# Decoder step on one core: gathering only the selected rows of the paged cache, and ranking the blocks earlier

## The reference

```
o_cmp, p   = attend(q, compressed keys, compressed values)   # one key per block
imp        = sum of p over the 4 query heads of the kv head
score      = imp, with blocks 0, 31 and 32 forced to the top
idx        = top_k(score, 16)                                # 16 of 33 blocks
o_sel      = attend(q, sel_k of the blocks in idx, sel_v of the blocks in idx)
o_win      = attend(q, last 512 window keys, values)
o          = g0 * o_cmp + g1 * o_sel + g2 * o_win
```

## Time and profile before

| | |
|---|---|
| median of 3 runs | 1637.56 us (1637.17 to 1639.81) |
| the profiled execution | 1638.89 us |
| its span, first to last instruction | 1637.1 us |
| busy: TensorE / VectorE / ScalarE | 1351.6 / 592.1 / 281.6 us |
| moved by DMA | 591.24 MB, mean 361 GB/s |
| the samples' phase on TensorE (first key transpose to first `w_o` matmul) | 449.7 to 558.7 us |

### The profile page before, as it was taken

How to read it: one execution, slowest core, us unless ns; L and a number is a source line. 1 busy time by engine, 2 the same in 40 slices (tenths; PEclk the granted TensorE clock), 3 DMA queues, 4 the chain that set the end, 5 groups by cost and what they waited for, 6 DMA issues and landing times.

```text
span 1637.1 us, 24667 instructions
## 1 busy us (share of the span) xinstructions
PE 1351.6 (83%) x10647; PEld 844.7 (52%) x10647; DVE 592.1 (36%) x1289; ACT 281.6 (17%) x660; POOL 90.5 (6%) x112
## 2 busy tenths in 40 slices
PE   8999999999999899996866788667785676676675
PEld 6887888888866588643323243333332232232332
DVE  2845566686686221382401212012120120120125
ACT  0013301201265010211110111101111011011113
POOL 1220011011231000010000000000000000000000
PEclk9999999999999999997977988889898797897888
DMA  9975476887789999479999999999999999999996
GB/s 347 376 272 197 166 278 222 315 318 263 278 332 409 341 306 361 180 305 423 426 426 426 428 412 427 426 427 426 414 426 429 426 427 426 428 426 426 427 427 249
DMA packets 139874, 591.24 MB, mean 361 GB/s; under 512 B 9056, under 2 KB 98672, under 8 KB 106864
## 3 DMA queue, kind: packets, MB, share of 16 engines
q1 hardware_dynamic: 122624, 497.70, 76.5%
q0 software_dynamic: 10432, 75.82, 11.9%
q10 hardware_dynamic: 6704, 16.08, 2.6%
HBM read 580.54 MB, written 17.45 MB: 365 GB/s over the span
## 4 chain that ended last, share of the span: by engine, by line
PE 56%; DMA 41%; DVE 1%; ACT 1%; issue 1%; DVEq 0%; SPq 0%; ACTq 0%
DMA arena<-in_w_up 36%; PE ps L710 22%; PE ps L2251 9%; PE ps L1437 7%; PE ps L2269 3%; PE ps L2218 3%; DMA arena<-in_w_down 2%; PE ps L1280 2%; DMA arena<-in_win_v 2%; PE ps L860 1%; PE ps L2278 1%; PE ps L1289 1%; PE ps L2224 1%; ACT arena L1712 1%; PE ps L2148 0%
## 5 line engine op out<-in xcount | busy, mean ns | idle before, releaser
L2251 PE MATMUL ps<-arena 128*32 128x256 f32 x4352 | 338.9, 481 | 236.9 <-DMA arena<-in_w_up 236.7
L2251 PEld LDWEIGHTS ps<-arena 128*32 128x32 f32 x4352 | 183.4, 137 | 408.1 <-issue 362.2
L710 PE MATMUL ps<-arena 128*128 128x264 f32 x1600 | 365.4, 386 | 0.0
L710 PEld LDWEIGHTS ps<-arena 128*128 128x128 f32 x1600 | 299.9, 190 | 49.6 <-issue 0.9
L1969 DVE TENSOR_TENSOR arena<-arena,ps 64x256 f32<-64x256 f32 x34 | 14.4, 424 | 474.4 <-ACT arena L1716 474.4
L2269 PE MATMUL ps<-arena 128*32 128x512 f32 x1088 | 125.9, 602 | 1.6 <-DMA arena<-in_w_down 1.1
L1437 PE MATMUL ps<-arena 128*128 128x264 f32 x512 | 118.2, 388 | 1.3 <-DMA arena<-in_w_o 1.3
L1716 ACT ACTIVATE arena<-ps 64x256 f32<-64x256 f32 x34 | 12.8, 375 | 566.2 <-PE ps L2251 566.2
L1437 PEld LDWEIGHTS ps<-arena 128*128 128x128 f32 x512 | 95.8, 190 | 20.7 <-issue 3.4
L2218 PE MATMUL ps<-arena 128*32 128x512 f32 (+1 forms) x816 | 98.5, 595 | 0.1
L1729 ACT COPY arena<-ps 32x512 f32<-32x512 f32 x128 | 73.7, 576 | 134.6 <-PE ps L2269 122.2
(11 more groups left out here) (481 smaller groups left out, 1125.0 us busy)
## 6 DMA issues: line engine op xcount, KB each, us to landing
arena<-in_w_up SPq DMA_DIRECT2D x61, 2048.0 KB, 34.1
arena<-in_w_gate SPq DMA_DIRECT2D x59, 2048.0 KB, 31.1
arena<-in_w_down SPq DMA_DIRECT2D x59, 2048.0 KB, 31.2
arena<-in_w_in SPq DMA_DIRECT2D x50, 1024.0 KB, 10.3
arena<-in_w_o SPq DMA_DIRECT2D x16, 1024.0 KB, 11.0
arena<-in_w_gate SPq DMA_DIRECT2D x10, 1024.0 KB, 30.7
arena<-in_w_down SPq DMA_DIRECT2D x10, 1024.0 KB, 31.2
arena<-in_w_up SPq DMA_DIRECT2D x6, 1024.0 KB, 31.1
```

Of the source, the lines that this page charges most:

```text
L710: last = pe.matmul(ps[:, n % 2, 0:T], ring[:, slot, k, cols], x[:, k, :], start=(k == 0), stop=(k == KT - 1))
L2251: last = pe.matmul(ps[BS * q:BS * q + BS, 0, 0:CHUNK // 2], xs[:, kk * 4 + i, :], w[:, at:at + CHUNK // 2], start=(k == 0), stop=(k == KT ...
```

## The change

1. **Rows skipped.** For pages 6 to 15 (keys of samples 6 and 7, all values) the row numbers come from `chosen_row`: the number of `seq_row`, plus 65,536 where neither head of the sample selects the row's block. The gather has a bounds check, and a row out of bounds is not fetched. The buffer keeps what was in it. GpSimd waits ahead of page 6 for `chosen_row` (`seq_ready` at 2).
2. **Ranking earlier.** VectorE no longer does `state(0)` and `state(1)` ahead of the ranking. Its order becomes: softmax, ranking, `state(0)`, gates, `chosen_row`, `state(1)`, `state(2)`, mask. TensorE's matmuls for `s_imp` go from step 5 to step 3, those for `s_selb` from step 8 to step 6. Two matmuls and three small VectorE instructions are added for `chosen_row`.
3. **Order at the end.** TensorE does `values(0)` right after the loop, ahead of `retained` and `turn_peaks(1)`, and the other pieces move one value matmul later. The results rotate through the PSUM banks (`value_bank`: samples 0 and 1 in bank 5, and 6 and 7 in bank 4, which the window scores hold until `peaks(1)`). VectorE does `state(6)` ahead of `shares(1)`.
4. **SyncE's order.** The windows of samples 6 and 7's values wait for pages 12 and 13 to land, `w_o` slices 0 and 1 for pages 14 and 15. `state_out(5)` moves behind the fourth `w_o` slice.

```
+UNCHOSEN = 2 ** 16
+FIRST_CHOSEN = 6
 def pages_in(pool, a, m, i):
+    page = m.pages[i % 4].rearrange("p a b -> p (a b)")
+    src, b = a["sel_k" if i < NS_TOK else "sel_v"], i % NS_TOK
+    if i < FIRST_CHOSEN:
...
+    else:
+        pool.indirect_dma_start(out=page, out_offset=None, in_=src,
+                                in_offset=bass.IndirectOffsetOnAxis(ap=m.chosen_row[:, b:b + 1], axis=0),
+                                bounds_check=src.shape[0] - 1, oob_is_err=False).then_inc(m.page_full[i % 4], 16)
...
+    value_bank = lambda b: 4 + (b // 2 + 1) % 4
...
@@ SyncE
         state_next(4)
-        state_out(5)
+        def page_landed(i):
+            sp.wait_ge(m.page_full[i % 4], 16 * (i // 4 + 1))
         for b in (6, 7):
+            page_landed(NS_TOK + b - 2)
             sp.wait_ge(S["s_vst"], b - 5)
             window_in(sp, a, m, NS_TOK + b)
-        final = 2 * NS_TOK - 1
-        sp.wait_ge(m.win_full[final % N_WIN], 16 * (final // N_WIN + 1))
-        sp.wait_ge(m.page_full[final % 4], 16 * (final // 4 + 1))
         for n in range(N_EARLY):
+            if n < 2:
+                page_landed(2 * NS_TOK - 2 + n)
             if n % 2 == 0 and n < 4:
                 sp.wait_ge(S["s_vst"], 5 + n // 2)
             if n == 4:
-                for b in (6, 7):
+                for b in (5, 6, 7):
                     state_out(b)
             project_in(sp, a, m, n)
@@ GpSimd
         for i in range(4, 12):
+            if i == FIRST_CHOSEN:
+                pool.wait_ge(front["seq_ready"], 2)
             pool.wait_ge(S["s_turned"], 10 * (i - 3))
             pages_in(pool, a, m, i)
@@ VectorE
-        v.wait_ge(S["s_v_in"], 2)
-        v.wait_ge(S["s_kq_in"], 2)
-        state(0)
         v.wait_ge(S["s_cexp"], 1)
...
-        state(1)
         v.wait_ge(S["s_imp"], 1)
...
-        v.tensor_scalar(selrow[0:16, :], selrow[0:16, :], float(TOPK), None, ALU.is_lt).then_inc(S["s_rank"], 1)
+        done.link(v.tensor_scalar(selrow[0:16, :], selrow[0:16, :], float(TOPK), None, ALU.is_lt))
+        v.tensor_copy(sel_wide.rearrange("p (b r) -> p b r", r=4), selrow[0:16, 0:NBLK].unsqueeze(2).broadcast_to([16, NBLK, 4])
+                      ).then_inc(S["s_rank"], 1)
+        v.wait_ge(S["s_v_in"], 2)
+        v.wait_ge(S["s_kq_in"], 2)
+        state(0)
+        v.wait_ge(S["s_in"], N_IN)
+        v.tensor_scalar(prob_c[0:64, :], prob_c[0:64, :], gate[0:64, 0:1], None, ALU.mult)
         v.tensor_tensor(rgn[0:64, :], gnr[0:64, :], m.rows[0:64, 0, :], ALU.mult)
+        v.wait_ge(S["s_selb"], 1)
+        done.link(v.tensor_scalar(m.chosen_row, ps[:, 3, 412:420], 0.5, float(UNCHOSEN), ALU.is_lt, ALU.mult))
+        v.tensor_tensor(m.chosen_row, m.chosen_row, m.seq_row, ALU.add).then_inc(front["seq_ready"], 1)
+        state(1)
         state(2)
-        v.wait_ge(S["s_selb"], 1)
...
+        state(6)
         shares(1)
-        state(6)
@@ TensorE
-            if i == 5:
+            if i == 3:
...
-            if i == 8:
+            if i == 6:
                 pe.wait_ge(S["s_rank"], 1)
...
+                of_sample = s_("to_half", 16).rearrange("r (h u kv g) -> r kv h u g", h=2, u=16, kv=2)
+                for kv in range(KV):
+                    last = pe.matmul(ps[:, 3, 412:420], sel_wide, of_sample[:, kv, :, 0:4, 0], start=(kv == 0), stop=(kv == 1))
                 last.then_inc(S["s_selb"], 1)
...
+        values(0)
         retained(range(0, 6))
         turn_peaks(1)
-        values(0)
+        values(1)
         turn_back(1)
-        values(1)
+        values(2)
         totals(1)
-        values(2)
+        values(3)
+        fold(0)
         turn_probs(1)
-        values(3)
         values(4)
-        fold(0)
         values(5)
```

More of the change, by code:

```diff
@@ L232 @@
 ENDS = tuple((name, value) for value, names in (
[L233 to L237, removed]
+    (1, "cw_ready c4_ready c4_in gl_done gl_ev gl_fold gates_in gl_wide s_rows s_rows_in pooled rows_ready s_v s_or "
+        "s_var s_std s_gated s_ft s_q s_kct s_kct_in s_c s_cexp s_cmax s_cprob s_imp s_rank s_selb"),
+    (2, "zero_ready seq_ready s_kq_in s_v_in s_peak s_mxt s_top s_back s_nm s_exp s_tot s_prob s_pt s_pt_a "
+        "s_pt_v s_out_a"),
     (3, "s_spread s_out_v"),
@@ L914, in pages_in @@
 def pages_in(pool, a, m, i):
-    name, b = (("sel_k", i) if i < NS_TOK else ("sel_v", i - NS_TOK))
-    pool.indirect_dma_start(out=m.pages[i % 4].rearrange("p a b -> p (a b)"), out_offset=None, in_=a[name],
-                            in_offset=bass.IndirectOffsetOnAxis(ap=m.seq_row[:, b:b + 1], axis=0)).then_inc(m.page_full[i % 4], 16)
+    page = m.pages[i % 4].rearrange("p a b -> p (a b)")
+    src, b = a["sel_k" if i < NS_TOK else "sel_v"], i % NS_TOK
+    if i < FIRST_CHOSEN:
+        pool.indirect_dma_start(out=page, out_offset=None, in_=src,
+                                in_offset=bass.IndirectOffsetOnAxis(ap=m.seq_row[:, b:b + 1], axis=0)).then_inc(m.page_full[i % 4], 16)
+    else:
+        pool.indirect_dma_start(out=page, out_offset=None, in_=src,
+                                in_offset=bass.IndirectOffsetOnAxis(ap=m.chosen_row[:, b:b + 1], axis=0),
+                                bounds_check=src.shape[0] - 1, oob_is_err=False).then_inc(m.page_full[i % 4], 16)
 def window_in(sp, a, m, i):
@@ L952, in phase_s @@
     stats, agg, std = w(6), w(2), w(1)
+    m.chosen_row = w(NS_TOK).bitcast(I32)
     w = Taker(arena, 32768, KVC)
@@ L1078, in keep_out @@
             act.wait_ge(S["s_vst"], 2 * q + 2)
-            A.copy(outs[:, 2 * q:2 * q + 2, :], ps[:, 4 + q, :].rearrange("p (b d) -> p b d", b=2)).then_inc(S["s_out_a"], 1)
+            A.copy(outs[:, 2 * q:2 * q + 2, :], ps[:, value_bank(2 * q), :].rearrange("p (b d) -> p b d", b=2)).then_inc(S["s_out_a"], 1)
         for i in range(2 * NS_TOK):
@@ L1324, in values @@
             pe.wait_ge(m.win_full[i % N_WIN], 16 * (i // N_WIN + 1))
-            out = [ps[32 * c:32 * c + 32, 4 + b // 2, cols] for c in range(4)]
+            out = [ps[32 * c:32 * c + 32, value_bank(b), cols] for c in range(4)]
             for j in range(4):
@@ L1382, in _ @@
                 last.then_inc(S["s_v"], 1)
-            if i == 5:
+            if i == 3:
                 pe.wait_ge(S["s_cprob"], 1)
                 pe.matmul(ps[0:16, 3, 0:256], s_("to_kv", 64), prob_c[0:64, :], start=True, stop=True).then_inc(S["s_imp"], 1)
-            if i == 8:
+            if i == 6:
                 pe.wait_ge(S["s_rank"], 1)
                 for h in (0, 1):
-                    last = pe.matmul(ps[:, 3, 336 + 33 * h:369 + 33 * h], s_("to_half", 16)[:, h * P:(h + 1) * P], selrow[0:16, :],
-                                     start=True, stop=True)
+                    pe.matmul(ps[:, 3, 336 + 33 * h:369 + 33 * h], s_("to_half", 16)[:, h * P:(h + 1) * P], selrow[0:16, :],
+                              start=True, stop=True)
+                of_sample = s_("to_half", 16).rearrange("r (h u kv g) -> r kv h u g", h=2, u=16, kv=2)
+                for kv in range(KV):
+                    last = pe.matmul(ps[:, 3, 412:420], sel_wide, of_sample[:, kv, :, 0:4, 0], start=(kv == 0), stop=(kv == 1))
                 last.then_inc(S["s_selb"], 1)
```

7 lines of the change are left out of this document (3 added, 4 removed).

## The result

| | before | after |
|---|---|---|
| median, us (20 runs each) | 1637.75 (1636.49 to 1640.87) | 1640.76 (1638.43 to 1644.55) |
| ratio to before, 95% interval | | 1.0016 [1.0009, 1.0023] |
| profiled execution, us (span) | 1638.89 (1637.1) | 1639.73 (1637.9) |
| `w_o` matmuls start, us | 558.69 | 558.76 |

The forecast was 1631.2. The changed kernel is 3.0 us slower by the medians: a difference that the interval separates from none, though it stays just inside the 3.3 us that the prediction counted as "the same". The samples' phase begins 1.3 us earlier in it (448.39 against 449.67), so the phase takes about 1.4 us longer.

What follows compares the result with a forecast made beforehand. Full DMA ahead of `w_o` was taken as the bound, with any shift of `w_o` reaching the end. 8.4 us gained minus 2.0 for late states gave 6.4, so a median of 1631.2 us, range 1628.6 to 1638.5.

Steps and rivals of the forecast that it cites:

- The frame: Experts' phase: as long as its bytes wherever it starts, so a shift of `w_o` reaches the end one for one.
- the walk: Values phase on TensorE, block by block: from `values(0)` at 520.0 to `w_o` at 550.3 us.
- Part 1: Skipped rows of the value pages and keys 6 and 7: 6.2 MB less, all 14.6 us of DMA time saved.
- the first rival: Last value pages: a page lands no sooner though smaller; 3.8 us gained, 1633.8 us; chance 0.18.
- Part 2: Key loop: ranking ends 7 us earlier, but the loop ends at 520.0 instead of 516.9, 3.1 us of delay.
- the sum: Key loop: the delays ahead of its end from the early ranking, together 3.1 us.
- Part 4: SyncE's state traffic comes late: 1 us at `state(3)`, 1 us behind `state(5)`, 2.0 us; bounds 0 and 8 us.
- The second rival: States take the pages' place: 15 us per `state_out`, VectorE stops 8 us at `state(5)`, 1637 us; chance 0.16.
- Part 3: Values: `values(0)` straight behind the loop, no DMA in the way, `w_o` at 550.3 against 558.69, 8.4 us gained.
- The third rival: Gather: a skipped row occupies its engine like a fetched one; everything lands 6 us later, 1643.6 us; chance 0.12.

Runs made afterwards that it cites:

- the skip alone: The kernel before with rows skipped in the eight value pages only, all else in the old order: 1636.53 us, ratio 0.9991.
- the lumped kernel: The kernel before, skipping 304 value rows by a fixed pattern that leaves half of the groups of four partitions whole: 1639.36 us, ratio 1.0002.
- rows spread: The kernel before with value rows skipped and the rows of two neighbouring blocks interleaved over partitions: 1632.56 us, ratio 0.9963.
- the even kernel: The kernel before, skipping 304 value rows by a fixed pattern that takes a row out of every group of four partitions: 1631.5 us, ratio 0.9961.
- The small outs: The changed kernel with neighbouring blocks' rows interleaved, `state_in(3)` ahead of `state_out(1)`, and only 128 columns of states 0 to 4 written: 1631.84 us, ratio 0.9963.
- the first experiment: The changed kernel with one swap in SyncE's order, `state_in(3)` issued ahead of `state_out(1)`: 1640.15 us, ratio 1.0011.

## Why the prediction was wrong

It missed by 9.6 us, outside its range and on the other side of no change. Two terms failed: the time that the skipped rows give back (taken as all of the 14.6 us, with 4.75 us measured) and the wait at `state(3)` (charged with 1 us, with 5.5 us measured). The frame around them held.

**The frame.** "Every microsecond by which `w_o` starts earlier or later reaches the end, one for one": from the start of `w_o` to the end of the span all fourteen kernels take 1078.3 to 1080.4 us, with starts from 549.8 to 564.8. That holds, so nearly all of the miss lies ahead of `w_o`. In the traces `w_o` comes 7.8 us late in the phase's own time. The phase began 1.3 us earlier, the rest took 0.7 us longer. The last 2.4 us are no step of the walk: the forecast took its profiled run to lie 1.3 us above the median as before, and it lies 1.0 us below.

**Part 1, the first step that failed.** Between nothing saved and "all its time saved (14.6 us)" the prediction took the latter, "since the stretch is bound by bytes". The bytes fell by the 6.2 MB forecast, but fetching them again costs 4.75 us (6.2 by the ratios). What was wrong is the step from the sum of bytes to the landing of a page: a page is whole only when its fullest engine is done, and the tail of the skip alone (share 0.03), the lumped kernel (0.50) and the 7.9 us between equal bytes show it. The prediction had the rule of the Trainium skill, and by it the first rival. Its argument against, "holes fall elsewhere in each" page, needs the engines to make up for one another over the queued pages. By that rule and the reference's selection one engine has no hole at all in the last four pages, which hold 88, 84, 80 and 96 rows (the prediction has "84 to 96").

**Part 2, right in its steps.** Page 6 left at 482.5 (forecast 483.1), page 7 at once, `peaks(0)` ended such that TensorE waited 0.4 us (0.7). The key loop's price without a stall of states is seen where the states are relieved: `values(0)` at 519.2 against 516.4 with the ranking at its old place, 2.8 us, where the sum had 3.1. "I cost this wait at nothing" for page 6 left out one thing: DMA is half idle meanwhile. Some 3.4 MB fewer moved between 470 and 490 than before, of which at most 1.3 MB are skipped. With page 6 issued at its old time 2.1 MB of them are back (304 and 330 GB/s); the other 1.3 MB fit SyncE's late list. What the wait costs in time stays open: the run with whole keys, which also fetches 1.3 MB more, is 1.4 us faster, with intervals that overlap.

**Part 4, the second step that failed.** "I charge 1 us at `state(3)` and 1 us behind `state(5)`: 2.0 us." The place and the mechanism were named, and the size was not: `state_in(3)` took 16.7 us, above the 14.3 us that was the largest row of before. The landing at "495 to 500" was 501.3, VectorE was ready for it at 495.8 and not at 497.3, and so lost 5.5 us. TensorE's wait of 7.5 us is that plus the 2.0 us of part 2, and the 20 transposes behind it took 1.8 us longer at the lower clock. Against the forecast's walk, `values(0)` came 6.3 us late once the phase's earlier start is taken off (525.0 plus 1.3, against 520.0). The second rival had "15 us per `state_out` under load" and put the stall at `state(5)`, giving 1637. That a state's transfers are slow beside pages and VectorE stops for one is what happened. The link was another: `state_out(0)` landed in 2.9 us, `state_in(3)` was held in SyncE's list by `state_out(1)` until 484.6, as part 4 had it, and was itself slow. A slow out (21.1 us) held an in back in the run with the in first, at `state(7)`. The rival was priced with all the pages' time saved, and so came out as a gain.

**Part 3, right but worth little alone.** The order of values gains nothing by itself (1632.73 against 1632.56): TensorE is at the last values sooner and waits for their pages. With SyncE's part of the change it is 2.4 us (on rows spread in both). From `values(0)` to `w_o` the forecast's walk had 30.3 us; the changed kernel took 33.8, of which 2.3 are the waits for pages 14 and 15 and 1.5 one block of values at the lower clock (3.45 us instead of 1.93). So 6.3 and 3.5, less the 2.0 charged, are the 7.8 us by which `w_o` missed the forecast in the phase's own time.

**The third rival** had the right side, and the saving (4.75 or 6.2 us) stands at its deciding point of 6 us. Its mechanism is not what was found. A row out of bounds does not occupy its engine like a fetched one: the even kernel, with 5.0 MB less, gains 7.3 us. It was on the right side for another reason. Its other half, DMA lost in front of page 6, is real, and its price is open.

**The sum as measured.** From before: skip alone 2.1 us gained, the orders of TensorE and SyncE bring it to 5.4, the early ranking and keys 6 and 7 take 8 back. That is 2.5 to 3 us slower. The forecast had charged the early ranking with 3.1 us in part 2 and 2.0 in part 4; with the ranking undone, and the late state with it, the sign turns.

Still open: how the 8 us of the early ranking divide between the late states, the idle DMA and the later issue of the last pages. The small outs relieve the chain but also leave out 2.3 MB, and no run changes the chain alone and keeps it short. Open too is why the medians differ by 2.2 us more than the profiled executions; single runs of one kernel spread over 2 to 8 us, those of the kernel before too (6.6 us over the 27 runs beside the first experiment). A fourth buffer for the states, which would cut the tie between out and in, was not tried.

## What to carry to other kernels

Work that is moved ahead on one engine pushes other work back, and what hangs on that (buffer free, out issued, out landed, next in issued, next in landed) must be walked to its last link. The largest landing time of before is no upper bound under the new load (14.3 us before, 16.7 after). Rows left out of the gather saved time here only where they relieved the fullest DMA engine (7.9 us between two kernels of equal bytes), so put the rows of one unit across the engines before counting the bytes. Holding back two windows and a state behind the pages needed first was worth as much here (2.6 us) as leaving out 4.9 MB (2.1 us).

## What was not expected of the hardware

- A skipped row is still a packet. Queue 0 has 10432 packets before and after. The packets under 512 B rose from 9056 to 9437: 381 more, beside 380 skipped rows.
- A page hardly landed sooner for having fewer rows: the last four value pages of the changed kernel (80 to 96 rows) took 9.8 to 16.8 us, pages 12 and 15 of before 10.4 and 19.6 with 128 rows. With the holes even over the groups of four partitions the last one took 11.0 us, with the same bytes lumped 18.4.
- A state of 0.5 MB took 16.7 us to land when it was issued just behind two pages (1.3 and 1.6 MB of rows fetched), and 4.1 us when it was issued 1.5 us ahead of the first of them. One took 2.9 us to leave at 478, at a DMA share of 0.49 in that stretch, and one 21.1 us beside value pages. At 425 GB/s it would be 1.2 us.
